# Hybrid decoder step on one core: the parts of the next expert job's token rows one half earlier, the gate's Silu behind the weight split

## What is computed

```python
def moe_swiglu(h, w_router, w_gate, w_up, w_down):
    xt = h.reshape(-1, d)
    logits = (xt @ w_router).astype(f32)
    top_v, top_i = lax.top_k(logits, TOP_K)                  # 2 of 8
    wts = jax.nn.softmax(top_v, axis=-1)
    comb = jnp.einsum('tk,tke->te', wts, jax.nn.one_hot(top_i, N_EXPERTS, dtype=f32))
    y = jnp.zeros(xt.shape, f32)
    for e in range(N_EXPERTS):
        he = jax.nn.silu(xt @ w_gate[e]) * (xt @ w_up[e])    # 1024 -> 3584
        y = y + comb[:, e:e + 1] * (he @ w_down[e])          # 3584 -> 1024
    return y
```

## Time and profile before

| | us |
|---|---|
| median of 3 runs | 2040.57 (2040.54 to 2041.18) |
| profiled execution | 2043.85, of which span 2042.1 |
| PE busy | 1822.7 (89%) |
| DVE busy | 1453.8 (71%) |
| ACT busy | 1169.6 (57%) |
| span of the nine jobs | 901.0 to 2015.2 |

### The profile page before, as it was taken

How to read it: one execution, slowest core, us unless ns; L and a number is a source line. 1 busy time by engine, 2 the same in 40 slices (tenths; PEclk the granted TensorE clock), 3 DMA queues, 4 the chain that set the end, 5 groups by cost and what they waited for, 6 DMA issues and landing times.

```text
span 2042.1 us, 25450 instructions
## 1 busy us (share of the span) xinstructions
PE 1822.7 (89%) x9047; PEld 1464.3 (72%) x9047; DVE 1453.8 (71%) x1380; ACT 1169.6 (57%) x1202; POOL 260.1 (13%) x316
## 2 busy tenths in 40 slices
PE   6797879999776776879999999999999999999995
PEld 2494679998633434858878787887878878787884
DVE  1335454520499997468888888888888888788887
ACT  1442244511444444457777776777777777777675
POOL 1003000000067774016000000000000000000001
PEclk8797589999856766989999999999999999999997
DMA  9744224333412213469999899998989999899995
GB/s 387 319 180 153 103 99 165 133 144 127 165 42 83 83 51 120 191 256 419 385 361 376 344 386 366 357 374 338 378 333 397 375 355 375 331 392 362 360 381 208
DMA packets 72277, 549.00 MB, mean 269 GB/s; under 512 B 8169, under 2 KB 8448, under 8 KB 15249
## 3 DMA queue, kind: packets, MB, share of 16 engines
q1 hardware_dynamic: 69186, 538.54, 67.7%
q0 software_dynamic: 2464, 8.35, 1.1%
q10 hardware_dynamic: 558, 1.21, 0.2%
HBM read 528.65 MB, written 19.44 MB: 268 GB/s over the span
## 4 chain that ended last, share of the span: by engine, by line
PE 74%; DVE 16%; DMA 3%; ACT 3%; issue 3%; POOL 0%; DVEq 0%; SPq 0%; ACTq 0%
PE bank L1634 72%; DMA ring<-in_dense_rows_dram 3%; DVE sq L1439 2%; PE bank L2041 1%; DVE arena L1446 1%; DVE w_lo L432 1%; DVE fT L1415 1%; DVE fT L1413 1%; DVE sq L1447 1%; DVE fT L1439 1%; ACT w_hi L427 1%; DVE rstd L1146 1%; DVE parts L1557 1%; DVE w_lo L383 0%; DVE fT L1447 0%
## 5 line engine op out<-in xcount | busy, mean ns | idle before, releaser
L1634 PE MATMUL bank<-w_hi,parts 128*128 128x512 f32 x3024 | 906.4, 395 | 29.0 <-DVE parts L1557 21.7
L432 DVE TENSOR_TENSOR w_lo<-ring,w_hi 128x2048 fp32r<-128x2048 f32 x327 | 747.8, 2289 | 143.1 <-ACT w_hi L427 142.7
L427 ACT ACTIVATE w_hi<-ring 128x2048 fp32r<-128x2048 f32 x327 | 626.3, 1918 | 192.9 <-PE bank L1634 192.8
L1634 PEld LDWEIGHTS bank<-w_hi,parts 128*128 128x128 f32 x3024 | 563.1, 189 | 154.3 <-DVE w_lo L432 37.4
L1634 PE MATMUL bank<-w_lo,parts 128*128 128x512 f32 x1512 | 550.4, 391 | 0.0
L1634 PEld LDWEIGHTS bank<-w_lo,parts 128*128 128x128 f32 x1512 | 285.6, 189 | 61.8
L1634 PE MATMUL bank<-parts,w_hi 128*128 128x264 f32 x1600 | 301.6, 290 | 21.9 <-DVE parts L1153 21.9
L1634 PEld LDWEIGHTS bank<-parts,w_hi 128*128 128x128 f32 x1600 | 254.8, 194 | 25.5 <-issue 20.0
L383 DVE TENSOR_TENSOR w_lo<-ring,w_hi 128x2048 fp32r<-128x2048 f32 x50 | 114.7, 2301 | 191.9 <-ACT w_hi L377 191.8
L1634 PE MATMUL bank<-parts,w_lo 128*128 128x264 f32 x800 | 230.4, 288 | 0.0
L1634 PE MATMUL bank<-arena 32*128 32x264 f32 (+7 forms) x386 | 134.5, 512 | 77.2 <-DVE arena L1448 35.4
(11 more groups left out here) (382 smaller groups left out, 1502.4 us busy)
## 6 DMA issues: line engine op xcount, KB each, us to landing
ring<-in_expert_rows_dram SPq DMA_DIRECT2D x330, 1024.0 KB, 5.2
ring<-in_dense_rows_dram SPq DMA_DIRECT2D x48, 2048.0 KB, 8.6
hT<-in_expert_rows_dram SPq DMA_DIRECT2D x55, 1024.0 KB, 5.4
ring<-in_dense_rows_dram SPq DMA_DIRECT2D x8, 1408.0 KB, 6.0
x_rows<-arena SPq DMA_DIRECT2D x1, 7168.0 KB, 19.5
y_rows<-arena SPq DMA_DIRECT2D x10, 512.0 KB, 6.4
arena<-x_rows SPq DMA_DIRECT2D x9, 512.0 KB, 6.5
ring<-in_dense_rows_dram SPq DMA_DIRECT2D x2, 1024.0 KB, 4.9
```

The costliest lines, as they stand in the source:

```text
L427: act.activation(hi_slots[SLOT_OF[h]], half_ring[h % HALVES], ACT.Copy).then_inc(hi_ready, 1)
L432: dve.tensor_tensor(lo_slots[SLOT_OF[h]], half_ring[h % HALVES], hi_slots[SLOT_OF[h]].bitcast(F32), ALU.subtract).then_inc(lo_ready, 1)
L1634: return pe.matmul(out, lhsT, rhs, start=start, stop=stop, skip_group_check=True)
```

## The change

It has four edits, all in the expert jobs.

1. ACT: in a step behind the second half of a gate, `split_hi` of half h+3 now stands ahead of the Silu, not behind it. The high part `ht_hi(c-1)` stays behind both.
2. ACT and DVE: the two pieces of `xg_hi` and `xg_lo` stand in steps 38 and 39 (`NH - 4`, `NH - 3`), where they stood in steps 39 and 40. In each step they follow the split.
3. `slot_free` is gone. For each half it waited for the last user of the same split buffer, which is the half three before it, and so the same count of the same semaphore as `half_free(j, h)` in the line behind it.
4. `SLOT_OF` is written as `h % 3`. The list before held 0, 1, 2 fourteen times, which is the same.

```diff
-        SLOT_OF = [i for n in (3,) * (NH // 3) for i in range(n)]
+        SLOT_OF = [h % AHEAD for h in range(NH)]
...
-        def slot_free(eng, j, h):
-            last = [n for n in range(h - NH, h) if SLOT_OF[n % NH] == SLOT_OF[h]][-1]
-            half_free(eng, j if last >= 0 else j - 1, last % NH)
...
                 for h in range(NH):
                     kind, c = kinds[h // 2]
                     to = half_after(j, h)
-                    slot_free(act, *to)
                     half_free(act, j, h)
+                    split_hi(act, *to)
                     if kind == "gate" and h % 2:
                         if c >= 2:
                             act.wait_ge(h_act_ready, NCHK * j + c - 1)
                         act.activation(g_act[:, c % 2, :], bank[2 * (c % 2)][:, :], ACT.Silu).then_inc(g_ready, 1)
-                    split_hi(act, *to)
-                    if kind == "gate" and h % 2 and c:
-                        ht_hi(c - 1)
+                        if c:
+                            ht_hi(c - 1)
                     if h == NH - 4:
                         ht_hi(NCHK - 1)
-                    if h in (NH - 3, NH - 2):
-                        xg_hi(j + 1, h - (NH - 3))
+                    if h in (NH - 4, NH - 3):
+                        xg_hi(j + 1, h - (NH - 4))
...
-                    slot_free(dve, *to)
                     half_free(dve, j, h)
...
                     split_lo(dve, *to)
                     if kind == "gate" and h % 2 and c:
                         ht_lo(c - 1)
-                    if h in (NH - 3, NH - 2):
-                        xg_lo(j + 1, h - (NH - 3))
+                    if h in (NH - 4, NH - 3):
+                        xg_lo(j + 1, h - (NH - 4))
```

More of the change, by code:

```diff
@@ L400, in hybrid_trunk @@
         lo_slots = [w[:, 0:HALF] for w in w_lo]
-        SLOT_OF = [i for n in (3,) * (NH // 3) for i in range(n)]
         AHEAD = 3
-        assert len(SLOT_OF) == NH
+        SLOT_OF = [h % AHEAD for h in range(NH)]
         def half_count(j, h):
```

## The result

| | us |
|---|---|
| before, median of 4 runs | 2040.59 (2040.54 to 2041.18) |
| changed, median of 4 runs | 2005.30 (2003.19 to 2006.56) |
| ratio | 0.9825, 95% interval 0.9808 to 0.9842 |
| forecast | 2008.0, range 2003.5 to 2014.5 |

The account below looks back on a forecast made before the run. PE was taken to bound the expert jobs, with waits around the seams. Seam 21.2, half 4 6.3 and clock 5.0 sum to 32.5 us, taking 2040.57 to 2008.0 us, range 2003.5 to 2014.5.

Parts of the forecast that it names:

- Seam, 8 x 2.65 = 21.2 us: Between jobs: earlier `xg_hi` and `xg_lo` remove PE's wait ahead of half 0, 2.65 us at each of eight seams.
- residual of 0.15: At the seam: PE still loses 0.15 us (0 to 0.3), since the weight load can't run ahead.
- rival B: At the seam: second `xg_lo` one DVE instruction late, 0.7 us on eight seams, 2013.6 us; chance 0.10.
- No cost at the loop's end: At the loop's end: PE's branch is over 3 us early and no fetch occurs, so no stall stays.
- Rival C: At the loop's end: an instruction fetch keeps the seam's gap and clock, saving only 6.3 us, 2034.3 us; chance 0.02.
- Half 4, 7 x 0.9 = 6.3 us: At job start: the split ahead of Silu and table load removes PE's 0.9 us loss at half 4, seven jobs.
- Half 5: After half 4 at job start: its split on DVE ends just in time for PE, costing 0 to 0.2 us.
- Mid-job splits, zero: In mid-job: six splits a job come 0.5 us earlier but fall into slack, gaining nothing.
- The doubled wait, zero: In the expert jobs: removing `slot_free` gains zero, since the doubled wait had no instruction.
- Clock, 5.0 us: Behind four of eight seams: idle PE drops its clock, 1.24 us each; filling the gap regains 5.0 us.
- Rival A: Behind seams: clock not regained, or timed runs had fewer falls than the profiled one, 2013.1 us; chance 0.12.
- Weight stream: In the jobs: the DMA rate rises from 367 to 378 GB/s without becoming the bound.

Follow-up runs that it names:

- run 2: Changed kernel with the `xg_hi` and `xg_lo` pieces back in steps 39 and 40, split still ahead of the Silu, `slot_free` out: 2034.39 us (0.9963).
- Run 3: Changed kernel with both pieces of `xg_hi` and `xg_lo` in step 39: 2012.86 us (0.9855).
- run 1: Changed kernel with the Silu ahead of the split again, pieces still in steps 38 and 39: 2016.01 us (0.9878).
- runs 7 and 8: Changed kernel with a one-column Silu heading each job: 2002.54 us (0.9813); the same with DVE copying both halves of y in the first loop: 2002.18 us (0.9812).
- run 5: Changed kernel with the split ahead of the Silu behind gate 0 only, Silu ahead in the six other steps: 2006.61 us (0.9826).
- run 4: Kernel before the change with 11 more matmuls at the end of each job, filling PE's wait at the seam: 2037.09 us (0.9974).
- run 6: Changed kernel with the second piece of `xg_hi` and `xg_lo` left in step 40, only the first in 38: 2032.15 us (one run).

## Why the prediction was right, point by point

- **Seam, 8 x 2.65 = 21.2 us.** Right, and slightly small. The gap went to nothing, where I had kept a residual of 0.15: I had reckoned that the second `xg_lo` would end 0.25 us before PE's next matmul, too late for the weight load to run ahead. It ended 0.32 us before it, and the load began 0.13 us behind that end, in time. The 0.07 us come from ACT, which started the split of half 0 at 1012.75, 4.36 us behind `turn_x`, against 4.44 before; by run 2 at least 0.06 of that is the doubled wait, whose effect I had put at nothing, so this part of the gain came by luck. So eight seams gave 8 x 2.8 = 22.4 us. The order of DVE that I wrote down is the one in the rows, and the first piece does lie in the idle time ahead of half 0. Run 3 shows that a piece 0.6 us later costs 0.53 us a seam, so the margin was real and thin, under 0.1 us (rival B lost by no more than that).
- **No cost at the loop's end.** Right: half 0 follows half 41 at the matmuls' own pace, and no queue but the data's has a packet in that stretch. Rival C is out.
- **Half 4, 7 x 0.9 = 6.3 us.** Right: 6.83 us by run 1, 7.7 by run 2, of which the doubled wait is 0.9; the first job gives 0.3 of it, for which I had counted nothing. Half 5 was just in time, as forecast (0 to 0.2 us): it cost some 0.08 us, by runs 7 and 8.
- **Mid-job splits, zero.** Right by run 5.
- **The doubled wait, zero.** Wrong in its reason and slightly in size. With it up to 39 instructions a job went from DVE and up to 7 from ACT. ACT now starts some 0.06 us earlier behind PE, and the gap at half 3 is 0.05 us shorter. That is 0.35 us in seven jobs beside the residual at the seam. No run takes `slot_free` out alone. That it is the cause rests on the seam of run 2 and on half 3 of run 1, where nothing else was changed; it is argued from those rows and not shown by a run of its own.
- **Clock, 5.0 us.** Right in cause, somewhat small: run 4 gives 5.6. I took one job's price (1.24 us) four times, while those behind the fourth and the last seam cost 1.6 each. Rival A was that the timed runs would not get this back; they saved 35.3 us and run 4's saved 4.4, so most of it is in them.
- **Weight stream.** It rose to 380 GB/s as forecast (378) at a share of 0.98, and ACT waited for no load: the mean rate is no bound yet, but the room is small.
- **The sum.** 22.4 + 6.8 + 5.6 = 34.8 of the 35.8 us by which the jobs got shorter; 0.3 more is at the tail (5.02 us of PE's wait against 5.37), and 0.35 is the gap at half 3, 0.05 us shorter in seven jobs (the doubled wait). The forecast 32.5 was short by the residual that didn't come (1.2), the clock (0.6), the first job's half 4 and the tail. The errors are small and mostly on one side. The profiled execution also shows 3.0 us less ahead of the jobs, where nothing was changed.

## What to carry to other kernels

When an engine waits at a seam, walk the queue of the engine that it waits for and look for an idle slot earlier in that queue: an operand whose input has long been ready may stand behind work that is itself held by the waiting engine, and here moving it across that work cost nothing. Price the idle time with what follows from it, the restart and the clock behind it; here these added 0.1 us to each gap and 5.6 us in all. Count the instructions that only wait before you put a doubled wait at nothing. In a loop, look where the activation tables are loaded: a load ahead of a copy that feeds the critical engine can be put where the engine has time.

## What the runs showed of the hardware that I had not expected

- The clock fell behind four of eight seams with gaps of 2.5 us (before, and run 2) and behind five with gaps of 2.3 us (run 6), and behind none with a gap of 0.27 us by the rows (run 3) or with the 2.5 us filled (run 4). A fall cost 1.2 or 1.6 us in the kernel before. Which seams it hit was not the same from kernel to kernel.
- A table load took 1.28 us, and the first loop paid it twice in each job, although the two functions can share a table: with a Silu first, the copies behind it caused no load (runs 7 and 8).
- A wait for a count that had already been reached still took an instruction of 17 ns on ACT or 21 ns on DVE, and with the doubled ones gone ACT started some 0.06 us earlier behind PE (run 2 against before).
- Half 0's weight load began 0.13 us behind the end of the piece that it needed, and then PE lost nothing (the change); with the piece 0.6 us later PE lost 0.53 us (run 3).
- The same instructions ahead of the jobs took 896.4 to 902.4 us in ten profiled executions. The granted clock was at 1.2 GHz for 314 to 338 us of them, and the one with the least (the change) was not the shortest. What decides that stays open.
